# One stage of products put between the steps of an attention: the delta rows' gate in a float32 transformer kernel

## The reference, cut to what matters

```python
y_a = rms_norm_2(o_a, dn_norm_w[l]).reshape(b, s, DN_WIDTH) * jax.nn.silu(za)
y_a = y_a @ w_proj_a[l]                      # 1024 x 1024: the row products
...
for gi, (win, dil) in enumerate(DIL_CONFIGS):     # 3 groups of 4 heads: dilations 1, 4, 16
    o_g, lse_g = dilated_window_attention(qb[:, :, hs], kb[:, :, hs], vb[:, :, hs], win, dil)
...
y_b = (o_b * w_g[..., None].astype(o_b.dtype)).reshape(b, s, ATTN_WIDTH) * jax.nn.silu(zb)
y_b = y_b @ w_proj_b[l]
merged = jax.nn.sigmoid(ga) * y_a + jax.nn.sigmoid(gb) * y_b
```

## Time and profile before

| | us |
|---|---|
| median of three runs (2052.59 to 2054.3) | 2054.08 |
| the profiled execution | 2055.86 |
| its span, from the first to the last instruction | 2054.1 |
| TensorE busy | 1974.9 (96%) |
| VectorE busy | 1118.2 (54%) |
| ScalarE busy | 839.8 (41%) |
| GpSimd busy | 366.6 (18%) |

### The profile page before, as it was taken

One profiled execution on the slowest core, in us unless ns is written; L12 is line 12 of the kernel. 1 busy time (PEld: TensorE's weight loads), 2 busy tenths in 40 slices (PEclk: granted clock), 3 DMA queues, 4 the chain that ended last, 5 costly groups with the idle time before them and its releaser, 6 DMA issues. The chain is left out here.

```text
span 2054.1 us, 27318 instructions
## 1 busy us (share of the span) xinstructions
PE 1974.9 (96%) x10418; PEld 1600.1 (78%) x10418; DVE 1118.2 (54%) x2036; ACT 839.8 (41%) x1744; POOL 366.6 (18%) x350
## 2 busy tenths in 40 slices
PE   8999999999999999899999999799999998999997
PEld 7776588888887878568888888688778887886686
DVE  5788644423434489835643553579775331525654
ACT  4455733322423344754321332454443334535632
POOL 1335800000000153750000000003030330004300
PEclk9999999999999999999999999999999999999999
DMA  6331023323332432013543533232225222341232
GB/s 193 90 86 52 2 75 109 103 93 93 93 112 72 121 102 74 20 42 113 186 152 103 174 103 114 72 103 82 82 78 160 76 69 93 95 140 42 75 131 81
DMA packets 177667, 198.27 MB, mean 97 GB/s; under 512 B 38899, under 2 KB 140930, under 8 KB 177026
## 3 DMA queue, kind: packets, MB, share of 16 engines
q1 hardware_dynamic: 177538, 196.53, 31.0%
HBM read 180.75 MB, written 11.55 MB: 94 GB/s over the span
## 5 line engine op out<-in xcount | busy, mean ns | idle before, releaser
L161 DVE TENSOR_TENSOR weight_pairs<-weight_ring,weight_pairs 128x1024 fp32r<-128x1024 f32 (+4 forms) x293 | 355.6, 1216 | 398.5 <-ACT weight_pairs L152 397.3
L182 PE MATMUL psum<-operand,weight_pairs 128*128 128x512 f32 x1320 | 526.9, 399 | 12.1 <-PEq L230 8.5
L152 ACT ACTIVATE weight_pairs<-weight_ring 128x1024 fp32r<-128x1024 f32 (+4 forms) x293 | 303.1, 1037 | 524.6 <-PE psum L184 509.5
L184 PE MATMUL psum<-operand,weight_pairs 128*128 128x512 f32 x1320 | 516.8, 391 | 0.0
L183 PE MATMUL psum<-operand,weight_pairs 128*128 128x512 f32 x1320 | 516.7, 391 | 0.0
L182 PEld LDWEIGHTS psum<-operand,weight_pairs 128*128 128x128 f32 x1320 | 248.9, 189 | 71.7 <-issue 18.6
L184 PEld LDWEIGHTS psum<-operand,weight_pairs 128*128 128x128 f32 x1320 | 248.5, 188 | 53.8
L183 PEld LDWEIGHTS psum<-operand,weight_pairs 128*128 128x128 f32 x1320 | 249.1, 189 | 50.6 <-issue 1.0
L915 POOL TENSOR_SCALAR probs<-probs,stats 128x128 f32<-128x128 f32 (+3 forms) x176 | 162.8, 941 | 223.6 <-DVE stats L817 222.2
L182 PE MATMUL psum<-weight_pairs,hidden 128*128 128x512 f32 x512 | 200.7, 392 | 0.0
L183 PE MATMUL psum<-weight_pairs,hidden 128*128 128x512 f32 x512 | 200.0, 391 | 0.0
(11 more groups left out here) (439 smaller groups left out, 2750.1 us busy)
## 6 DMA issues: line engine op xcount, KB each, us to landing
weight_ring<-in_w_in_dram SPq DMA_DIRECT2D x100, 512.0 KB, 3.7
weight_ring<-in_w_up_dram SPq DMA_DIRECT2D x64, 512.0 KB, 3.7
weight_ring<-in_w_down_dram SPq DMA_DIRECT2D x64, 512.0 KB, 3.5
weight_ring<-in_w_out_dram SPq DMA_DIRECT2D x24, 512.0 KB, 3.5
ada_rows<-in_ada_w_dram SPq DMA_DIRECT2D x24, 512.0 KB, 4.6
spilled<-v_t SPq DMA_DIRECT2D x22, 256.0 KB, 3.3
weight_ring<-in_w_in_dram SPq DMA_DIRECT2D x20, 256.0 KB, 2.8
weight_ring<-in_w_proj_a_dram SPq DMA_DIRECT2D x8, 512.0 KB, 3.5
```

The costliest lines, as they stand in the source:

```text
L152: act.activation(self.pairs[:, i % SPLIT_RING, 0, 0:n], self.buf[:, i % RING, 0:n], ACT.Copy).then_inc(self.rounded, 1)
L161: dve.tensor_tensor(self.pairs[:, i % SPLIT_RING, 1, 0:n], self.buf[:, i % RING, 0:n], self.pairs[:, i % SPLIT_RING, 0, 0:n].bitcast(F32), ...
L182: pe.matmul(out, lhs[0], rhs[0], start=start, stop=False)
L184: return pe.matmul(out, lhs[1], rhs[0], start=False, stop=stop)
```

## The change

The row products are no stage of their own any more. `row_gate_products` now returns three generators, and `attention` (its new argument `dense`) draws one piece from each in every step: TensorE a slice of 6 matmuls behind the scores (and one slice ahead of step 0), 32 slices in all; ScalarE the high half of a weight item, and VectorE the low half of it, in every fourth step, and VectorE the product with the gate in steps 6, 9, 14, 17, 22, 25 and 30 and once behind the loop. The products use two banks only, 6 and 7 (h = 0 and 1). A pair of chunks takes 8 slices: for its first item two slices on h = 0 and two on h = 1, the same for its second item. The banks are written anew in slices 8p and 8p + 2, which wait for the product with the gate of the pair of chunks before. TensorE issues slice s + 1 in step s. To free the two banks, both turned tiles of a pair share bank 4, ScalarE copies them in one instruction (`copy_pair`) and VectorE none, and the values of all runs use bank 5. Without `dense` (the attentions of the first block) nothing changes.

```diff
-    split_copies = besides is None
+    split_copies, pair_copies = besides is None and dense is None, dense is not None
-    TB, OUT = 4, 6
+    TB, OUT, N_OUT = (4, 6, 2) if dense is None else (4, 5, 1)
+    def turned_bank(j, w):
+        return psum[:, TB + j % 2, 0:w] if dense is None else psum[:, TB, S // 2 * (j % 2):S // 2 * (j % 2) + w]
...
-            if run >= 2 and 2 * p % RUN == 0:
-                pe.wait_ge(stored_low if in_pairs else stored, run - 1)
+            if run >= N_OUT and 2 * p % RUN == 0:
+                pe.wait_ge(stored_low if in_pairs else stored, run - N_OUT + 1)
...
+        slices = None if dense is None else dense["pe"](pe)
+        if dense is not None:
+            next(slices)
...
             if p < pairs:
                 scores(p)
+            if dense is not None:
+                next(slices, None)
...
+        def copy_pair(p):
+            j = 2 * p
+            w = jobs[j].width
+            act.wait_ge(turned, j + 2)
+            if p >= 2:
+                act.wait_ge(valued, j - 2)
+            act.activation(probs_t[:, j % 4:j % 4 + 2, 0:w], psum[:, TB, :].rearrange("p (h c) -> p h c", h=2)[:, :, 0:w],
+                           ACT.Copy).then_inc(copied_act, 1)
...
-            if 0 <= p - TURN < pairs:
+            if pair_copies and 0 <= p - TURN < pairs:
+                copy_pair(p - TURN)
+            elif 0 <= p - TURN < pairs:
                 copy(2 * (p - TURN))
...
+            if dense is not None:
+                next(slices, None)
             if at_run(p, STORE) is not None:
                 store(at_run(p, STORE))
+        if dense is not None:
+            finish_woven(slices)
...
     start = weights.taken
-    end = start + KD
-    times_done, = part.sems("rows", "times_done")
-    block = part.block
-    @block.sync
+    BANK, SLICES = 6, KD
+    first_done, gated = part.sems("rows", "first_done gated")
+    @part.block.sync
     def _(sp):
-        weights.send(sp, end)
-    @block.tensor
-    def _(pe):
+        weights.send(sp, start + KD)
+    def products(pe):
         pe.wait_ge(*pair_ready)
-        for c in range(0, KD, 2):
-            pe.wait_ge(*bank_free[c // 2])
-            product_by_channels(pe, psum, ((c + 4) % 8, (c + 5) % 8), weights, pair, KD)
-    @block.scalar
-    def _(act):
-        for c in range(KD):
-            weights.high(act, start + c + 1)
-    @block.vector
-    def _(dve):
-        for c in range(KD):
-            weights.low(dve, start + c + 1)
-            dve.wait_ge(weights.items_done, start + 2 * (c // 2) + 2)
+        pe.wait_ge(*bank_free)
+        for p in range(KD // 2):
+            for i in range(2):
+                w = weights.take(pe)
+                for h in range(2):
+                    if i == 0 and p:
+                        pe.wait_ge(gated, 2 * (p - 1) + h + 1)
+                    for kk in range(KD // 2):
+                        k = i * (KD // 2) + kk
+                        mm = product(pe, psum[:, BANK + h, :], [w[j][:, kk, h * P:(h + 1) * P] for j in (0, 1)],
+                                     [pair[:, k, j, :] for j in (0, 1)], start=(k == 0), stop=(k == KD - 1))
+                        if kk == KD // 2 - 1:
+                            if h:
+                                weights.used(mm)
+                            elif i:
+                                mm.then_inc(first_done, 1)
+                        if kk % 2:
+                            yield
+    def high(act):
+        for p in range(KD // 2):
+            for m in range(SLICES):
+                if m % (SLICES // 2) == 0:
+                    weights.high(act, start + 2 * p + 2 * m // SLICES)
+                yield
+    def rest(dve):
+        def gate(c):
             dve.wait_ge(gate_ready, c + 1)
-            dve.tensor_tensor(merged[:, c, :], psum[:, (c + 4) % 8, :], merged[:, c, :], ALU.mult).then_inc(times_done, 1)
-    return times_done
+            dve.tensor_tensor(merged[:, c, :], psum[:, BANK + c % 2, :], merged[:, c, :], ALU.mult).then_inc(gated, 1)
+        for p in range(KD // 2):
+            for m in range(SLICES):
+                if m % (SLICES // 2) == 0:
+                    weights.low(dve, start + 2 * p + 2 * m // SLICES)
+                if m == 1 and p:
+                    dve.wait_ge(weights.items_done, start + 2 * p)
+                    gate(2 * p - 1)
+                if m == 3 * SLICES // 4:
+                    dve.wait_ge(first_done, p + 1)
+                    gate(2 * p)
+                yield
+        dve.wait_ge(weights.items_done, start + KD)
+        gate(KD - 1)
+    return dict(pe=products, act=high, dve=rest)
```

More of the change, by code:

```diff
@@ L680, in attention @@
 def attention(block, psum, jobs, stores, ident, ident_half, probs, probs_t, stats, sems, besides=None, ready={},
-              freed=None, turns_ready=(), values_ready=(), held=None, fill=None):
+              freed=None, turns_ready=(), values_ready=(), held=None, fill=None, dense=None):
     (scored, found, shifted, powered, inverted, normed, turned, copied_act, copied_dve, valued, stored, stored_low,
@@ L727, in turn @@
                         pe.wait_ge(copied_dve, p)
-                    elif split_copies:
+                    elif split_copies or pair_copies:
                         pe.wait_ge(copied_act, p)
@@ L732, in turn @@
                 for b in range(jobs[j].width // P):
-                    mm = pe.transpose(psum[:, TB + j % 2, b * P:(b + 1) * P],
+                    mm = pe.transpose(turned_bank(j, jobs[j].width)[:, b * P:(b + 1) * P],
                                       probs[:, j % PB, b * P:(b + 1) * P], ident[:])
@@ L745, in values @@
                 pe.wait_ge(copied_dve, p + 1)
+            elif pair_copies:
+                pe.wait_ge(copied_act, p + 1)
             else:
@@ L751, in values @@
                 for h, j in enumerate(pair):
-                    mm = pe.matmul(psum[64 * h:64 * h + 64, OUT + run % 2, tile], jobs[j].values[b],
+                    mm = pe.matmul(psum[64 * h:64 * h + 64, OUT + run % N_OUT, tile], jobs[j].values[b],
                                    probs_t[:, j % 4, b * P:(b + 1) * P], start=(b == 0), stop=(b == nb - 1))
@@ L821, in store_low @@
             high, _, low = stores[run]
-            dve.tensor_tensor(low, psum[:, OUT + run % 2, :], high.bitcast(F32), ALU.subtract).then_inc(stored_low, 1)
+            dve.tensor_tensor(low, psum[:, OUT + run % N_OUT, :], high.bitcast(F32), ALU.subtract).then_inc(stored_low, 1)
+        slices = None if dense is None else dense["dve"](dve)
         count, step, needed, picked = besides or (0, None, 0, None)
@@ L887, in store @@
             out, bank_view, _ = stores[run]
-            act.activation(out, bank_view(psum[:, OUT + run % 2, :]), ACT.Copy).then_inc(stored, 1)
+            act.activation(out, bank_view(psum[:, OUT + run % N_OUT, :]), ACT.Copy).then_inc(stored, 1)
+        slices = None if dense is None else dense["act"](act)
         for p in range(pairs + STORE + 1):
-            if 0 <= p - TURN < pairs:
+            if pair_copies and 0 <= p - TURN < pairs:
+                copy_pair(p - TURN)
+            elif 0 <= p - TURN < pairs:
                 copy(2 * (p - TURN))
@@ L2993, in second_part @@
                     ident, sb("o_stats", [P, 4, T * H], ctx), y, q, k, v, KB)
-                times_done = row_gate_products(merge, psum, weights, y_pair, (low, H), merged, gate_ready,
-                                               ((v_stored, KB), (v_stored, KB), (stored, 3 * KB), (stored, 3 * KB)))
+                row_gates = row_gate_products(merge, psum, weights, y_pair, (low, H), merged, gate_ready, (v_stored, KB))
                 scores_done, powers_done, scores_turned = dilated_attention(
-                    merge, {0: ((stored, 3 * KB), (v_stored, KB))}, (times_done, (KD - 2, KD)), psum, q, k, v, y, stats, KB,
+                    merge, {0: ((stored, 3 * KB), (v_stored, KB))}, row_gates, psum, q, k, v, y, stats, KB,
                     window_incl_half, causal_half, residues_half, ident, ident_half, sb)
@@ L3182, in projected_and_gated, with dilated_attention @@
     return stored, v_stored, low, gate_ready
-def dilated_attention(part, ready, freed, psum, q, k, v, y, stats, C, window_incl, causal, residues, ident, ident_half, sb):
+def dilated_attention(part, ready, dense, psum, q, k, v, y, stats, C, window_incl, causal, residues, ident, ident_half, sb):
     jobs = []
@@ L3203, in dilated_attention @@
         attention(part.block, psum, jobs, stores, ident, ident_half, sb("probs2", [P, 8, 2 * P], c2),
-                  sb("probs_t2", [P, 4, 2 * P], c2), stats, sems, None, ready, freed)
+                  sb("probs_t2", [P, 4, 2 * P], c2), stats, sems, None, ready, dense=dense)
     scored, powered, turned = sems[0], sems[3], sems[6]
```

## The result

| | before | changed |
|---|---|---|
| median, us | 2053.76 (2052.59 to 2054.30, 4 runs) | 2065.30 (2064.69 to 2065.94, 4 runs) |
| profiled execution, us | 2055.86 | 2065.94 |
| its span, us | 2054.1 | 2064.2 |
| the two stages, to the first product of the next | 87.49 | 99.58 |
| from there to the merge of the groups | 31.87 | 31.74 |

The ratio is 1.0055, with a 95% interval of 1.0042 to 1.0068: slower by 11.5 us. The forecast was 2070.0, so 15.9 slower.

A forecast was written before the change was run, and what follows sets the result against it. TensorE, almost full in both stages, was taken as the bound. 43.5 + 31.7 + 3.2 + 13.8 + 3.1 + 8.1 = 103.4 us instead of 87.5, 15.9 more, gave 2070.0 us, range 2054 to 2080.

The forecast's parts named there:

- The three waits for the gate: TensorE waits for VectorE's product with the gate before slices 10, 18 and 26: 5.1, 4.9 and 3.8, together 13.8 us.
- The output bank: Values of a new run wait for ScalarE's eviction in steps 13 and 21: 1.3 and 1.8, together 3.1 us.
- One bank for the turned probabilities costs nothing that I can find: Attention's transposes sharing one bank: no cost, since before a transpose also waited for the copy of the previous pair.
- The clock: TensorE's clock drops to half around each of the three long waits: 2.7 us each, 8.1 in all.
- Bare work and seams: Both stages with no wait: row products 43.5, attention 31.7, seams of 32 slices 3.2; 78.4 us.
- Behind the stages: Second gate's stage, up to the merge of the groups: taken as 0, with bounds of -6.3 and +2 us.
- rival A: The waits on TensorE are there but its clock stays up: 2062 us, chance 0.18.
- C: Rival: chain to the gate about half as long, 2 to 3 us a wait, clock holds: 2053, no change, chance 0.08.
- B: Rival: product with the gate is done when TensorE reaches slices 10, 18 and 26: 2045 us, chance 0.12.
- D: Rival: TensorE's clock swings between half and full through the whole stretch: 33.9 us more, 2088, chance 0.05.

The follow-up runs named there:

- e1: Changed kernel with VectorE's product with the gate of chunks 1, 3 and 5 one step earlier, ahead of the low half: 2049.75 us, ratio to before 0.9977.
- e8: Changed kernel with VectorE's low half one step later, behind the product with the gate of that step: 2052.47 us, ratio to before 0.9991.
- e7: e3 with SyncE issuing the last weight item behind the load of the gate rows, not ahead of it: 2048.01 us, ratio to before 0.9972.
- e9: Kernel before with only the joined copy (both turned tiles in one bank, copied by ScalarE), row products their own stage: 2057.87 us, ratio 1.0015.
- e3: Changed kernel with both moves, gate ahead of the low half and eviction ahead of the high half: 2049.23 us, ratio to before 0.9978.
- e5: Kernel before with only the bank edits (joined copy with its one bank, single output bank), row products their own stage: 2069.92 us, ratio 1.0075.
- e12: The kernel of e5 profiled once more, one execution on another chip: 2072.50 us.
- e10: Kernel before with only the single output bank for the values, row products their own stage: 2061.15 us, ratio 1.0028; its profiled execution 2055.26.
- e11: The kernel of e10 profiled once more, one execution on another chip: 2066.35 us.
- e6: e3 with the last two evictions (from step 27 on) behind the high half again: 2048.69 us, ratio to before 0.9972.
- e2: Changed kernel with ScalarE's eviction of a finished run ahead of the high half, nothing else: 2068.61 us, ratio to before 1.0070.
- e4: Changed kernel with high and low halves two steps later, in the third step of every four: 2073.13 us, ratio to before 1.0092.

## Why the prediction was right

- *The three waits for the gate* (13.8 in the forecast): 12.0, in the places and with the releaser named. Shown as the cause by e1, which takes off 15.6 us of stage with one move, and by e8, which takes off 14.2 by moving the low half alone. Mis-sized by 1.8, because I put the links end to end. The engines overlap them: the high half starts 0.68 us after the first exponential (I had 0.8), the gate 0.66 us after the maxima begin (I had 0.85 with shifts and reciprocal), and from the copy's start to the product there are 4.8 us where my links from the copy on make 5.4.
- *The output bank* (3.1): 2.4. Right as a term of this sum, with the sign and in two places. As a price of that edit it would be wrong: the waits behind gate waits were hidden, as predicted, and e1, which removes the cover, shows five of them with 5.8 us by weight loads, as the 2.4 are counted (3.6 by matmuls).
- *"One bank for the turned probabilities costs nothing that I can find"*: with products between the steps no run separates it; it can be no more than a part of the 2.9 us by which e7's stage of 81.3 lies above 78.4. In a stage without products the sentence is wrong: e9 is 3.0 us slower than before, with small waits of the scores and transposes and 4 us of half clock.
- *The clock* (8.1): 7.1. The mean of 2.7 a drop was 2.4; the first drop lasted 3.5 us, the other two 6.7 each, the first 1.4 and 1.1 us of these inside the wait.
- *Bare work and seams* (78.4): 78.1. e7, with no wait over 0.6 us, takes 81.3, of which weight loads waited about 3.8 for other engines in small pieces.
- *Behind the stages* (0): the way to the merge was 31.74 for 31.87. The merge began 11.6 us later than before. Half clock behind its wait lasted 3.3 us for 6.6, which gave back about 1.7, and so the span grew by 10.1 only. The load of the gate rows was issued at 1920.71, as late as I had said. Its cover was thinner than I had written: e3 shows that this load decides the merge as soon as the stage gets shorter.
- *The total.* Against the profiled executions I was 5.8 us high (15.9 for 10.1): 3.8 in the stage (103.4 for 99.6), 1.7 behind the merge. The medians lie 11.5 apart, which leaves 4.4. No term was too small, so the errors added up. By the time alone rival A (2062) is nearer to 2065.3 than my forecast (2070.0), so the number doesn't decide between them. (The range was to begin at C, which I put at 2053 in one place and at 2054 in the other.)

The rivals: A (clock stays up) falls by the windows, with 0.51, 0.50 and 0.50 at the three waits, and by e1, whose stage shrank by 6.6 us more than its waits. B, the waits absent, is what e7 makes of the program: 78.4 was its stage, 81.3 is measured, and 2048 is 3 us above its 2045. C was not what happened, though e8 is close to it in size: short waits, the clock holds, 2052.5. D, by the rule of the Trainium skill (TensorE: Matmul & The Clock Gate, "A second HAM failure mode: psum-queue depth-cycling"), fails for the changed kernel, where half clock goes with the three long waits alone, and for e1, whose 84 us with small waits are at 1.00. But I dismissed it too broadly. e5 and e12 are the same attention without products between its steps, with waits of up to 1.4 us, and there half clock lasted for 20 us and more. The row I used against the rule had gaps of 0.4 us and less, and said nothing of longer ones: the drop in e12 came behind 0.68 us. That the products between the steps are what kept the clock up in e1 and e8 is not shown: e5 and e12 differ from them in more than that, and the prediction had not named it as a reason.

## What to carry to other kernels

When work of one stage is put between the steps of another, write down for each reused bank who frees it, and place that instruction ahead of the pieces of that step whose results are needed only later: here one swap on VectorE was worth 15.6 us. Sum the chain by starts of instructions and not by their lengths, and when the stage gets shorter, ask which load behind it is now late. Where a kernel's executions spread more than those of the kernel beside it, look at the granted clock of more than one execution before giving its time a cause.

## What the runs showed of the hardware that was not expected

- Waits of the same number and length (5.2 us in five, the longest 1.3 to 1.4) left TensorE at full clock in one execution (e10) and at half clock for 3.4 and 13.6 us in another of the same kernel (e11, on another chip). The ten timed runs of e10 on one chip spread from 2055.3 to 2063.1 us, for 2052.0 to 2056.9 in twenty of the kernel before beside them.
- With six 512-column products in each step, waits of up to 1.55 us left the clock at 1.00 through the whole stage where they were the longest (e1, e3, e6, e7, e8), and with waits of 3.3 us and more there was half clock each time (the changed kernel, e2, e4). In e4 a wait of 1.55 us, 9 us behind one of 3.54, was followed by it too: from 1858.9 to 1862.7 the clock was 0.55. The next short one, 1.37 us at 1891.6, was not. Without the products a wait of 1.15 us came just ahead of 24 us of it (e5), and one of 0.68 us ahead of 34 us (e12).
- The two bank edits cost 3.0 and 6.3 us alone and 15.8 together. The waits for the eviction are the same with the joined copy and without it (5.2 us in e5, 5.3 in e10). What differs is the clock: behind the hand-over's half clock, and up to the merge, it is at half for 4 us in e9, for none and 17 us in e10 and e11, and for 24 and 34 us in e5 and e12.
